# Two-layer transformer block in split float32: the last two input-projection chunks as one seven-product Strassen unit

## The reference

```python
for l in range(DEPTH):                       # 2 layers
    h = rms_norm(x, attn_pre_g[l])           # 512 x 1024
    proj = h @ w_in[l]                       # 1024 x 3080
    qa, ka, va, qb, kb, vb, f_logit = jnp.split(proj, split_at, axis=-1)   # six of 512 columns, one of 8
    # rotary on qa, ka; differential attention on qa, ka, va; forgetting attention on qb, kb, vb
    x = x + rms_norm(mixed @ w_out[l], attn_post_g[l])
    h = rms_norm(x, ffn_pre_g[l])
    x = x + rms_norm((silu(h @ w_gate[l]) * (h @ w_up[l])) @ w_down[l], ffn_post_g[l])
```

## Time and profile before

| what | value |
|---|---|
| median of 3 runs | 2107.34 us (2105.56 to 2108.14) |
| the profiled execution, its own time | 2107.81 us |
| its span, first to last instruction | 2106.0 us |
| around the span | 1.8 us |
| PE busy | 2061.6 us (98% of the span) |
| DVE, ACT, POOL busy | 54%, 43%, 28% |
| read from memory | 174.76 MB, 84 GB/s over the span |
| mean granted PE clock | 0.997 of full |

### The profile page before, as it was taken

One profiled execution on the slowest core, in us unless ns is written; L12 is line 12 of the kernel. 1 busy time (PEld: TensorE's weight loads), 2 busy tenths in 40 slices (PEclk: granted clock), 3 DMA queues, 4 the chain that ended last, 5 costly groups with the idle time before them and its releaser, 6 DMA issues.

```text
span 2106.0 us, 31405 instructions
## 1 busy us (share of the span) xinstructions
PE 2061.6 (98%) x12462; PEld 1795.2 (85%) x12462; DVE 1146.7 (54%) x1784; ACT 915.1 (43%) x1556; POOL 598.2 (28%) x438
## 2 busy tenths in 40 slices
PE   7999999999999999999999999999999999999999
PEld 6886789999887886789999887877788889999987
DVE  6417558776305117558776306477566445877700
ACT  4226454455324126454455325455534434545611
POOL 3540030000544440030000543444466441000252
PEclk9999999999999999999999999999999999999999
DMA  5330023332323330023332331211211232333232
GB/s 193 100 110 1 2 90 104 98 121 91 112 94 98 98 100 1 1 90 103 99 120 91 110 95 55 82 59 50 61 51 51 101 100 81 101 101 111 86 114 72
DMA packets 129143, 178.80 MB, mean 85 GB/s; under 512 B 10163, under 2 KB 78062, under 8 KB 129006
## 3 DMA queue, kind: packets, MB, share of 16 engines
q1 hardware_dynamic: 128414, 175.24, 26.3%
q10 hardware_dynamic: 592, 1.64, 0.2%
HBM read 174.76 MB, written 2.10 MB: 84 GB/s over the span
## 4 chain that ended last, share of the span: by engine, by line
PE 42%; issue 42%; POOL 7%; DVE 6%; ACT 2%; DMA 0%; POOLq 0%; DVEq 0%; ACTq 0%
PE PS L1795 10%; PE PS L1797 10%; PE PS L1796 10%; POOL w_lo L649 7%; PE PS L2127 2%; PE PS L2102 2%; PE PS L2247 1%; PE PS L2086 1%; DVE nmax L1403 1%; PE PS L2037 1%; PE PS L2223 1%; PE PS L2215 1%; PE PS L1849 1%; PE PS L2109 0%; DVE R L1413 0%
## 5 line engine op out<-in xcount | busy, mean ns | idle before, releaser
L649 POOL TENSOR_TENSOR w_lo<-R,w_hi 128x1024 fp32r<-128x1024 f32 x168 | 404.4, 2416 | 1184.9 <-ACT w_hi L742 1125.7
L1795 PE MATMUL PS<-w_hi,xt_hi 128*128 128x512 f32 x928 | 375.3, 404 | 10.6 <-DVE R L1604 4.3
L1795 PE MATMUL PS<-xt_hi,w_hi 128*128 128x256 f32 (+1 forms) x1216 | 367.3, 302 | 0.0
L742 ACT ACTIVATE w_hi<-R 128x1024 fp32r<-128x1024 f32 (+1 forms) x180 | 183.4, 1029 | 423.2 <-PE PS L1797 422.8
L1797 PE MATMUL PS<-w_hi,xt_lo 128*128 128x512 f32 x928 | 364.3, 393 | 0.0
L1796 PE MATMUL PS<-w_lo,xt_hi 128*128 128x512 f32 x928 | 363.5, 392 | 0.0
L1797 PE MATMUL PS<-xt_hi,w_lo 128*128 128x256 f32 (+1 forms) x1216 | 361.8, 298 | 0.0
L1796 PE MATMUL PS<-xt_lo,w_hi 128*128 128x256 f32 (+1 forms) x1216 | 361.6, 297 | 0.0
L1796 PEld LDWEIGHTS PS<-xt_lo,w_hi 128*128 128x128 f32 x1216 | 233.0, 192 | 6.9 <-issue 1.0
L1795 PEld LDWEIGHTS PS<-xt_hi,w_hi 128*128 128x128 f32 x1216 | 233.0, 192 | 7.0 <-issue 1.0
L1797 PEld LDWEIGHTS PS<-xt_hi,w_lo 128*128 128x128 f32 x1216 | 232.9, 192 | 6.5
(11 more groups left out here) (299 smaller groups left out, 3546.2 us busy)
## 6 DMA issues: line engine op xcount, KB each, us to landing
R<-in_w_in SPq DMA_DIRECT2D x56, 512.0 KB, 3.8
R<-in_w_down SPq DMA_DIRECT2D x40, 512.0 KB, 3.4
UW<-in_w_gate SPq DMA_DIRECT2D x36, 512.0 KB, 4.0
UW<-in_w_up SPq DMA_DIRECT2D x36, 512.0 KB, 5.0
raw<-in_w_in SPq DMA_DIRECT2D x36, 512.0 KB, 3.7
R<-in_w_out SPq DMA_DIRECT2D x24, 512.0 KB, 3.3
R<-in_w_ffn_down SPq DMA_DIRECT2D x20, 512.0 KB, 3.4
UW<-in_w_ffn_gate SPq DMA_DIRECT2D x18, 512.0 KB, 4.0
```

Source lines behind the costliest of these rows:

```text
L649: nc.gpsimd.tensor_tensor(w_lo[:, r, 0:subs, :], raw_of(stage, lap)[:, r, 0:subs, :], w_hi[:, r, 0:subs, :].bitcast(F32), ALU.subtract).th ...
L742: nc.scalar.activation(w_hi[:, r, 0:subs, :], raw_of(stage, lap)[:, r, 0:subs, :], ACT.Copy).then_inc(hi_ready, 1)
L1795: mm(out_, a_hi, b_hi, start=start, stop=False, **kw)
```

## The change

In `in0` and `in1` the chunks KB and VB (columns 2048 to 3071 of `w_in[l]`) are no longer two laps. The stage has four laps, and then one unit, a Strassen-Winograd product of 2 × 2 blocks. The weights are cut into V11, V12 (k blocks 0 to 3 of KB's and VB's columns) and V21, V22 (k blocks 4 to 7), each 128 × 2048 floats, 1 MB; the tokens into A11, A12 (tokens 0 to 255, features k 0 to 3 and 4 to 7) and A21, A22 (tokens 256 to 511).

- SP (`load_wide`, after the loads of lap 3): waits for `evac[0]` of chunk 2, loads V11, V12, V21, V22, waits for the rest of the last product (`wu_lo`), and then goes on to the gain row G (layer 0) and the first slots of `out{l}`.
- DVE (`wide_front`, ahead of the copy of chunk 3): four sums hi + lo of tokens, four combinations S1 to S4 and their rests (each 128 × 1024); the rest of P1's weights, V12 − V11, V22 − that, that − V11 (each 128 × 2048). Then the copy of chunk 3, then (`wide_unit`) the rests of the other products, one more combination, and the sums and copies into KB and VB.
- ACT (`wide_unit`): rounds the four S, the weights of each product in the order P1, P7, P6, P2, P5, P4, P3 (128 × 2048 each, in alternating pairs of slots), copies two PSUM banks to two others twice (so that later products add onto them), two banks to `v_p7`, two to KB. The first lap of `out{l}` is rounded after that, slots 0 and 1 once P3 is used, slots 2 and 3 once P4 is.
- PE: seven products of 24 matmuls each of 512 columns, tokens stationary. P1 waits for its weights' rest, P7 also for `evac[1]` of chunk 3 and the rests of S.
- POOL has no part in the unit.

```diff
...
 HALF = SEQ // 2
+WIDE_P1, WIDE_P7, WIDE_P6, WIDE_P2, WIDE_P5, WIDE_P4, WIDE_P3 = range(1, PRODUCTS + 1)
 STAGES = []
 for _l in range(DEPTH):
-    STAGES += [(f"in{_l}", 6), (f"out{_l}", 2), (f"ffn{_l}", CLASSIC), (f"down{_l}", 6)]
+    STAGES += [(f"in{_l}", 4), (f"out{_l}", 2), (f"ffn{_l}", CLASSIC), (f"down{_l}", 6)]
 STAGES += [("in2", 11), ("branch2", 2), ("out2", 2), ("ffn2", CLASSIC), ("down2", 6)]
...
+        V11, V12, V21, V22 = (wide_f(a, 4, CW) for a in (8208, 10384, 24576, 26624))
+        v_t2 = wide_f(21168, 4, CW)
+        WIDE_HI = {"S1": 19120, "S2": 16560, "S3": 14512, "S4": 12464}
+        WIDE_LO = {"S1": 20144, "S2": 23216, "S3": 15536, "S4": 13488}
+        v_s_hi = {n: wide_r(a, 4, HALF) for n, a in WIDE_HI.items()}
+        v_s_lo = {n: wide_r(a, 4, HALF) for n, a in WIDE_LO.items()}
+        v_s_f = {n: wide_f(a, 4, HALF) for n, a in WIDE_LO.items()}
+        v_x = {n: wide_f(WIDE_HI[m], 4, HALF) for n, m in (("A11", "S4"), ("A12", "S1"), ("A21", "S3"), ("A22", "S2"))}
+        X_PART = {"A11": (slice(0, 4), slice(0, HALF)), "A12": (slice(4, KD), slice(0, HALF)),
+                  "A21": (slice(0, 4), slice(HALF, SEQ)), "A22": (slice(4, KD), slice(HALF, SEQ))}
+        v_p7 = wide_f(8208 + 2 * CW, 2, CW)
+        pair_hi = [w_hi[:, 2 * n:2 * n + 2].rearrange("p r s n -> p (r s) n") for n in range(2)]
+        pair_lo = [w_lo[:, 2 * n:2 * n + 2].rearrange("p r s n -> p (r s) n") for n in range(2)]
+        WIDE_SOURCE = {WIDE_P1: V11, WIDE_P7: V11, WIDE_P6: v_t2, WIDE_P2: V21, WIDE_P5: V12, WIDE_P4: v_t2, WIDE_P3: V22}
...
                 sp.wait_ge(u_lo, PRODUCTS * (UNITS * (FFN_AT[stage] + 1) - 1) + LO_E)
+            def load_wide(l):
+                stage = f"in{l}"
+                sp.wait_ge(evac[0], SET0[stage][0] + 2)
+                for half, parts in enumerate(((V11, V12), (V21, V22))):
+                    for n, dst in enumerate(parts):
+                        if half:
+                            sp.wait_ge(lo_ready, 4 * (LAP0[stage] + 3) + 2 * n + 2)
+                        sp.dma_start(dst, w_in[l][half * 4 * P:half * 4 * P + 4 * P, (4 + n) * CW:(5 + n) * CW]
+                                     .rearrange("(k p) n -> p k n", p=P)).then_inc(wide_in[half], 16)
+                sp.wait_ge(wu_lo, PRODUCTS * (l + 1))
             load_x([0, 1])
...
                         load_lap(stage, LAP0[stage] + chunk, chunk, 0)
+                    if stage in ("in0", "in1"):
+                        load_wide(int(stage[-1]))
             sp.wait_ge(final_ready, 1)
...
                         act.wait_ge(w_used, 4 * (lap - 1) + r + 1)
+                    if stage in ("out0", "out1") and isinstance(lap, int) and lap == LAP0[stage]:
+                        act.wait_ge(wu_used, PRODUCTS * int(stage[-1]) + (WIDE_P3 if r < 2 else WIDE_P4))
                     if is_down(stage) and isinstance(lap, int) and lap == LAP0[stage]:
...
                 return last
+            def wide_unit(l):
+                def used(product):
+                    act.wait_ge(wu_used, PRODUCTS * l + product)
+                def rounded(product):
+                    pair = (product - 1) % 2
+                    nc.scalar.activation(pair_hi[pair], WIDE_SOURCE[product], ACT.Copy).then_inc(wu_hi, 1)
+                last = LAP0[f"in{l}"] + 3
+                act.wait_ge(ws_made, 4 * (l + 1))
+                for name in ("S3", "S2", "S1", "S4"):
+                    nc.scalar.activation(v_s_hi[name], v_s_f[name], ACT.Copy).then_inc(ws_hi, 1)
+                act.wait_ge(wide_in[0], 32 * (l + 1))
+                act.wait_ge(w_used, 4 * last + 2)
+                rounded(WIDE_P1)
+                act.wait_ge(wt_made, 4 * l + 3)
+                act.wait_ge(w_used, 4 * last + 4)
+                rounded(WIDE_P7)
+                used(WIDE_P1)
+                rounded(WIDE_P6)
+                nc.scalar.activation(PS[:, 2:4, :], PS[:, 0:2, :], ACT.Copy).then_inc(w_p1_put, 1)
+                used(WIDE_P7)
+                act.wait_ge(wide_in[1], 32 * (l + 1))
+                rounded(WIDE_P2)
+                act.wait_ge(wu_lo, PRODUCTS * l + WIDE_P7)
+                nc.scalar.activation(v_p7, PS[:, 6:8, :], ACT.Copy).then_inc(w_p7_out, 1)
+                used(WIDE_P6)
+                rounded(WIDE_P5)
+                nc.scalar.activation(PS[:, 4:6, :], PS[:, 2:4, :], ACT.Copy).then_inc(w_u2_put, 1)
+                used(WIDE_P2)
+                act.wait_ge(wt_made, 4 * l + 4)
+                rounded(WIDE_P4)
+                nc.scalar.activation(KB[:, 0:2, :], PS[:, 0:2, :], ACT.Copy).then_inc(w_c11, 1)
+                used(WIDE_P5)
+                rounded(WIDE_P3)
             def attention1(l):
...
                     hi_lap(stage, LAP0[stage] + lap)
+                wide_unit(l)
                 hi_first(f"out{l}")
...
                 link(V.tensor_tensor(t2, r[2], r[3], ALU.add))
+            def wide_lo(l, product):
+                pair = (product - 1) % 2
+                dve.wait_ge(wu_hi, PRODUCTS * l + product)
+                V.tensor_tensor(pair_lo[pair], WIDE_SOURCE[product], pair_hi[pair].bitcast(F32),
+                                ALU.subtract).then_inc(wu_lo, 1)
+            def wide_front(l):
+                dve.wait_ge(ts_lo, TS0[f"in{l}"] + 2 * KD)
+                for name in ("A21", "A22", "A11", "A12"):
+                    ks, tok = X_PART[name]
+                    V.tensor_tensor(v_x[name], xt_hi[:, ks, tok].bitcast(F32), xt_lo[:, ks, tok].bitcast(F32),
+                                    ALU.add).then_inc(wx_made, 1)
+                dve.wait_ge(wx_made, 4 * l + 4)
+                V.tensor_tensor(v_s_f["S1"], v_x["A21"], v_x["A22"], ALU.add).then_inc(ws_made, 1)
+                V.tensor_tensor(v_s_f["S3"], v_x["A11"], v_x["A21"], ALU.subtract).then_inc(ws_made, 1)
+                dve.wait_ge(ws_made, 4 * l + 1)
+                V.tensor_tensor(v_s_f["S2"], v_s_f["S1"], v_x["A11"], ALU.subtract).then_inc(ws_made, 1)
+                dve.wait_ge(ws_made, 4 * l + 3)
+                V.tensor_tensor(v_s_f["S4"], v_x["A12"], v_s_f["S2"], ALU.subtract).then_inc(ws_made, 1)
+                for n, name in enumerate(("S3", "S2", "S1", "S4")):
+                    dve.wait_ge(ws_hi, 4 * l + n + 1)
+                    V.tensor_tensor(v_s_lo[name], v_s_f[name], v_s_hi[name].bitcast(F32), ALU.subtract).then_inc(ws_lo, 1)
+                dve.wait_ge(wide_in[0], 32 * (l + 1))
+                wide_lo(l, WIDE_P1)
+                V.tensor_tensor(V12, V12, V11, ALU.subtract).then_inc(wt_made, 1)
+                dve.wait_ge(wide_in[1], 32 * (l + 1))
+                dve.wait_ge(wt_made, 4 * l + 1)
+                V.tensor_tensor(v_t2, V22, V12, ALU.subtract).then_inc(wt_made, 1)
+                dve.wait_ge(wu_lo, PRODUCTS * l + WIDE_P1)
+                dve.wait_ge(wt_made, 4 * l + 2)
+                V.tensor_tensor(V11, v_t2, V11, ALU.subtract).then_inc(wt_made, 1)
+            def wide_unit(l):
+                def used(product):
+                    dve.wait_ge(wu_used, PRODUCTS * l + product)
+                wide_lo(l, WIDE_P7)
+                wide_lo(l, WIDE_P6)
+                dve.wait_ge(wu_lo, PRODUCTS * l + WIDE_P6)
+                V.tensor_tensor(v_t2, V21, v_t2, ALU.subtract).then_inc(wt_made, 1)
+                wide_lo(l, WIDE_P2)
+                wide_lo(l, WIDE_P5)
+                dve.wait_ge(wu_lo, PRODUCTS * l + WIDE_P5)
+                V.memset(VB[:, :, :, HD:HD + 1], 1.0)
+                wide_lo(l, WIDE_P4)
+                used(WIDE_P5)
+                dve.wait_ge(w_p7_out, l + 1)
+                V.tensor_tensor(VB[:, 2:4, :, 0:HD], heads(PS[:, 4:6, :], 8), heads(v_p7, 8), ALU.add).then_inc(w_c22, 1)
+                wide_lo(l, WIDE_P3)
+                used(WIDE_P4)
+                dve.wait_ge(w_c11, l + 1)
+                dve.wait_ge(w_c22, l + 1)
+                V.tensor_tensor(KB[:, 2:4, :], PS[:, 2:4, :], v_p7, ALU.add).then_inc(evac[0], 1)
+                used(WIDE_P3)
+                V.tensor_copy(VB[:, 0:2, :, 0:HD], heads(PS[:, 4:6, :], 8)).then_inc(evac[1], 1)
             def attention1(l):
                 stage = f"in{l}"
-                dst = (QA, KA, VA, QB, KB, None)
-                for c in range(6):
+                dst = (QA, KA, VA, QB)
+                for c in range(4):
+                    if c == 3:
+                        wide_front(l)
                     chunk_done(stage, c)
                     src = banks(c % 2)
-                    if c == 5:
-                        V.tensor_copy(VB[:, :, :, 0:HD], heads(src, 8)).then_inc(evac[1], 1)
-                    elif c >= 2:
+                    if c >= 2:
                         V.tensor_copy(dst[c], src).then_inc(evac[c % 2], 1)
                         if c == 2:
-                            V.memset(VB[:, :, :, HD:HD + 1], 1.0)
                             V.memset(decay, 0.0)
...
                         rotary(dst[c])
+                wide_unit(l)
```

(46 more changed lines are left out.)

## The result

Before: median 2107.66 us of five runs (2105.56 to 2108.14). After: 2118.83 us (2116.55 to 2119.81), ratio 1.0057 with a 95% interval of 1.0047 to 1.0068 (the quotient of the two medians is 1.0053). The kernel became slower by 11.2 us; the forecast was slower by 7.8, 2115.1 us, with a range up to 2119.5. The sign and the main places are right, the size is 3 to 4 us too small: two terms of the forecast fail, the sum to the last product, which was too low, and the attention's start, which was put at nothing. The profiled execution of after is the fastest of its five, 2116.55 us with a span of 2114.4; the others have spans of 2116.1 to 2117.7.

A forecast was written before the change was run, and what follows sets the result against it. PE, busy 98% of the span, was taken to bound the kernel. Per layer 0.5 to the last product, 2.1 clock and 1.3 behind the unit made 3.9, twice +7.8 us: 2115.1 us, range 2110.3 to 2119.5.

The forecast's parts named there:

- the sum to the last product: Per layer, up to the unit's last product: 5.44 us saved against waits of 0.1 and 5.9 us, +0.5 us.
- the attention's start: Start of the attention units, behind the gate sums: no term in the sum; a further clock fall only in rival 3.
- The work removed: On PE, per layer: 168 matmuls instead of 192, the 24 saved worth 5.44 us.
- P7 waits 5.9 us: Between P1 and P7: PE stands still 5.9 us per layer while DVE makes combinations, chunk 3's copy and P7's rest.
- The clock, 2.1 us: In P7, behind PE's wait: the clock falls to half, costing 2.1 us per layer, bounds 0 to 3.2.
- Rival 1: At P7: the clock holds through the wait; both layers 2110.9 us, chance 10%; one layer 2113.0, chance 5%.
- Behind the unit, 1.3 us: From the unit's end to the gate sums: late copy and POOL's block together +1.3 us per layer, bounds 0 to 2.4.
- (a): Behind the unit: late ACT roundings delay the forget logits' copy, 0.8 us in layer 0, 0.1 to 0.2 in layer 1.
- (b): Behind the unit: POOL's rests block L1368 and delay four copies, ending 1.3 us late; this takes in (a).
- Rival 2: Behind the unit: nothing lost, because the attention's start has slack; +5.2 us, 2112.5 us, chance 7%.
- rival 3: Clock low longer (3.2 us), or late items bring a further fall at the attention's start; up to 2119.5 us, chance 12%.
- Rival 4: Before P7: DVE serves P7 in time, so no wait; −8.3 us, 2099.1 us, chance 4%.

The follow-up runs named there:

- e1: The changed kernel run once more, unchanged: 2118.24 us, ratio 1.0050 to the kernel before.
- e4: Changed kernel with token sums, S and combinations made earlier and the four weight blocks loaded one chunk earlier: 2101.49 us, ratio 0.9974 to the kernel before.
- e7: Changed kernel with the copy of chunk 3 moved from DVE to ACT: 2117.68 us, ratio 1.0056 to the kernel before.
- e2: Changed kernel with 24 unread matmuls of 512 columns between P1 and P7: 2112.63 us, ratio 1.0026 to the kernel before.
- e9: Changed kernel with the edits of e2, e3 and e5 together: 2108.35 us over eleven runs, ratio 1.0007 to the kernel before.
- e3: Changed kernel with POOL's last rest behind the unit waiting until the forget gates are done: 2115.32 us, ratio 1.0042 to the kernel before.
- e6: Changed kernel with the edits of e3, e4 and e5 together: 2096.89 us, ratio 0.9953 to the kernel before.
- e5: Changed kernel with G and the first two output-weight slots loaded ahead of P3's rest: 2117.72 us, ratio 1.0055 to the kernel before.
- e8: Changed kernel with the edits of e3 and e5 together: 2113.81 us, ratio 1.0035 to the kernel before.

## Why the prediction was right in sign and 3 to 4 us too small

By its steps, per layer, with e1 beside the forecast:

- **The work removed**, 5.44 us: right. e4 gets 5.2 of it as soon as nothing waits.
- **P1 waits 0.1 us**: 0.25 in after. Right in kind.
- **P7 waits 5.9 us**: 5.7 by the trace, and 5.96 by the starts (11.40 us from P1's first matmul to P7's, less 5.44). Right. But the copy of chunk 3, "now queued behind them", was not what made it long: e7 took it out and gained 0.14 us, since ACT's rounding, which the forecast had ready 0.3 us earlier, takes nearly the same time.
- **No other wait in the unit**: right. But the sum to the last product, "+0.5 us per layer", came out as 1.1 (e2 and e9, where the clock plays no part), 1.1 us too little over the two layers. It is the largest part of the error. Per layer 0.15 us are P1's wait, 0.06 P7's, another 0.06 went when 0.56 was rounded to 0.5, and 0.3 are the pace: 0.2289 us for a matmul in e2's six products behind the wait against the 0.2267 that was taken from the earlier trace rows. In e4, where nothing waits, it is 0.2281, so most of the slower pace belongs to the unit itself. Where it comes from stays open.
- **The clock, 2.1 us**: 2.6 and 1.9 in e1, on average 2.25. The fall was forecast rightly. That the size came so near is in part luck: it was taken from another stage, and over the six executions with the wait it varies from 1.8 to 2.8 us. Rival 1, a clock that holds, is out. With the rule of the Trainium skill (TensorE: Matmul & The Clock Gate, Part 1: The HAM clock gate), that activity alone lifts the clock, the traces agree: a low stretch comes with every such wait and with none that was filled.
- **Behind the unit, 1.3 us**: 1.34 and 1.16 in e1. The late copy (a) gave 1.05 us of wait in layer 0 of after and 1.27 in e1, where 0.8 was forecast, and none in layer 1; with the block (b) L1368 took 1.29 us in layer 0 of after, 0.99 in e1, and 2.31 in layer 1 of both. Rival 2 is out. With the Trainium skill (SBUF — State Buffer, Who interferes with whom), that the engine which issues first holds the shared port, the traces agree: L1368 took 2.31 us when a rest of POOL had just begun, 0.18 when POOL was held back in e3. The case in which L1368 falls between two rests by itself did not come up.
- **Transfers, nothing**: right.

Two steps failed, then. One is **the sum to the last product**, sized at 0.5 and measured at 1.1 us a layer. The other is a term put at nothing, **the attention's start**: the sum has no term for it, and it came up only in rival 3, with 12% and as an upper bound. By the marks, this stretch takes 6.37 us with no fall (6.7 in e4 and e6), 7.1 to 7.4 with 3.4 us of low clock, and 8.5 to 8.8 with 6.8 us. Before had 3.4 us in both layers. After and e1 have none and 6.8, together +0.9 and +0.8 us; e5 had 6.8 twice, +2.8. So beside their lateness, the late items may have moved work around a fall of the clock by which that stretch swings 2.4 us a layer; that they did is not shown.

The sum for e1 is 2 × 1.1 for the unit, 4.5 for its clock, 2.5 behind it and 0.8 at the attention's start, 10.0 of 10.1; the forecast had 2 × 0.5, 4.2, 2.6 and 0, 7.8. The time around the span adds 0.4 (2.2 us against 1.8). What is left between e1's 10.5 and the 11.2 of the first comparison, 0.7 us, is within the spread of the runs (2115.61 to 2119.81 for this one kernel).

In rival 3 the text speaks of "1.6 more" for a further fall and the sum in brackets has 1.1; with 1.6 its end would be 2 × 6.6 = 13.2 us, 2120.5.

Rival 4, the only faster case, named the right turning point, "DVE serves P7 in time", and priced it at −8.3 us. By a rearrangement that this change does not contain, e4 and e6 came to −5.6 and −9.5. In e4's trace the unit and the stretch behind it make −10.4 + 2.4 = −8.0 us, which is rival 4's price; the 2 us that are missing went to the clock elsewhere.

## What to carry to other kernels

An algorithm that saves an engine's instructions has to be paid for by the preparation in front of it: write down the dependent chain up to the first operand (here three combinations, a rounding and a rest) beside the time until it is due, and if it doesn't fit, start it earlier before judging the algorithm. The same unit was worth +11 us with its chain started one chunk late and −5.6 us with it started in time. When PE is stopped for several microseconds, price the slower clock behind the stop as well, here another 2 us, and leave room for stretches further on whose low clock comes and goes (here up to 2.4 us each).

## What the runs showed that I had not expected

- In the windows of these traces the low clock came in stretches of 3.4 or 6.8 us. Behind the unfilled wait of 5.7 us it was 6.8 us each time, in both layers of all six executions (after, e1, e3, e5, e7, e8). What varies is how much of it falls into the wait, from 0.8 us in e3's layer 0 to 2.9 in after's layer 1, and the cost with it, 2.8 and 1.8 us by the distance from the copy of chunk 2 to E, against e2.
- The attention's start had 0, 3.4 or 6.8 us of low clock with nearly the same code before it. All five stretches of 6.8 us follow gate sums that came 13.3 to 13.4 us behind E, after 1.18 us of idle PE (layer 1 of after, e1 and e7, both layers of e5); but layer 1 of e2 and of e4 had the same and 3.4 us. What decides it I did not find. Whether it differs between executions of one kernel is not shown: the two profiled ones of after have the same pattern.
- At the program's start, before the first fall, the column PEclk reads 1.00 although the matmuls are 0.43 us apart, the pace of the low level (in before up to 17.5 us). There the distance of the starts tells the level, not the column.
- Twenty-four matmuls whose results nobody reads made the kernel 5.6 us faster (e2); in the traces 4.5 us are at P7.
- POOL and DVE stretch each other: a DVE operation of 0.18 us took 2.31, a pass of 1.22 took 3.42; where PE does not wait for them it costs nothing.
